# Feed-forward gate and up as one 512-column product: both halves of the input side by side, summed by VectorE

## The reference

```python
D_FF = 2816
def swiglu(xn, w_gate, w_up, w_down):
    return (jax.nn.silu(xn @ w_gate) * (xn @ w_up)) @ w_down
h = h + swiglu(rmsnorm(h, ffn_norm[l]), w_gate[l], w_up[l], w_down[l])   # l = 0, 1
```

## Time and profile before

| | us |
|---|---|
| median of 3 runs | 1963.29 (1955.23 to 1964.63) |
| profiled execution | 1963.11 |
| its span | 1961.3 |
| TensorE busy | 1734.0 (88%) |
| VectorE busy | 1019.6 (52%) |
| ScalarE busy | 510.2 (26%) |

### The profile page before, as it was taken

One profiled execution on the slowest core, in us unless ns is written; L12 is line 12 of the kernel. 1 busy time (PEld: TensorE's weight loads), 2 busy tenths in 40 slices (PEclk: granted clock), 3 DMA queues, 4 the chain that ended last, 5 costly groups with the idle time before them and its releaser, 6 DMA issues.

```text
span 1961.3 us, 22190 instructions
## 1 busy us (share of the span) xinstructions
PE 1734.0 (88%) x7497; PEld 1181.4 (60%) x7497; DVE 1019.6 (52%) x2438; ACT 510.2 (26%) x1012; POOL 279.1 (14%) x264
## 2 busy tenths in 40 slices
PE   7998999889989999799999899968878889788876
PEld 4784999856648999587565468543434434344332
DVE  1234555533435554445734311377776667776765
ACT  1342444212324443143211001122222212222222
POOL 0000000000000000000000000045434343333540
PEclk8999999999998999899999999989989999898998
DMA  5253566501336565133322325099999999999996
GB/s 173 77 169 103 167 192 183 167 16 44 96 103 181 180 184 182 31 126 124 105 110 80 115 78 189 25 371 420 420 421 421 422 421 421 421 421 421 422 421 255
DMA packets 209713, 435.30 MB, mean 222 GB/s; under 512 B 11649, under 2 KB 145153, under 8 KB 175745
## 3 DMA queue, kind: packets, MB, share of 16 engines
q0 software_dynamic: 36864, 268.45, 33.0%
q1 hardware_dynamic: 171760, 166.06, 26.5%
q10 hardware_dynamic: 1040, 0.13, 0.0%
HBM read 433.53 MB, written 1.05 MB: 222 GB/s over the span
## 4 chain that ended last, share of the span: by engine, by line
PE 72%; DMA 16%; DVE 7%; issue 3%; ACT 1%; POOL 0%; DVEq 0%; SPq 0%; POOLq 0%; ACTq 0%
PE ps L484 40%; DMA OT<-in_peer_uv,IX 15%; PE ps L1220 11%; PE ps L645 6%; PE ps L925 3%; PE ps L938 2%; PE ps L515 2%; PE ps L549 1%; PE ps L490 1%; PE ps L1135 1%; DVE SLOT L2277 1%; PE ps L1017 1%; DVE AR L1992 1%; PE ps L556 1%; DMA XT<-in_w_pq_by_head 0%
## 5 line engine op out<-in xcount | busy, mean ns | idle before, releaser
L1595 POOL DMA_INDIRECT SLOT<-in_peer_uv,IX x128 | 136.1, 1064 | 1520.2 <-DVE IX L2271 1276.0
L1220 PE MATMUL ps<-SLOT,AR 128*128 128x512 f32 x512 | 263.8, 671 | 96.6 <-ACT AR L1549 96.6
L484 PE MATMUL ps<-ARH 128*128 128x256 f32 x2112 | 261.0, 286 | 7.6 <-DVE ARH L1710 7.6
L484 PEld LDWEIGHTS ps<-ARH 128*128 128x128 f32 x2112 | 260.2, 195 | 9.5 <-issue 7.9
L1220 PEld LDWEIGHTS ps<-SLOT,AR 128*128 128x128 f32 x512 | 108.1, 216 | 245.9 <-issue 129.6
L2277 DVE SCALAR_TENSOR_TENSOR SLOT<-SLOT,V 128x1024 f32<-128x1024 f32 x128 | 153.3, 1224 | 77.4 <-DMA SLOT<-in_peer_uv,IX 75.4
L484 PE MATMUL ps<-XT,SLOT 128*128 128x256 f32 x832 | 183.2, 380 | 2.2 <-DVE XT L1659 1.3
L1710 DVE TENSOR_TENSOR ARH<-SLOT,ARH 128x2048 fp32r<-128x2048 f32 (+1 forms) x88 | 154.1, 1756 | 49.3 <-ACT ARH L1298 32.5
L484 PEld LDWEIGHTS ps<-XT,SLOT 128*128 128x128 f32 x832 | 157.4, 190 | 25.2 <-issue 3.7
L1220 PE MATMUL ps<-AR 128*128 128x512 f32 x320 | 144.6, 601 | 12.1 <-ACT AR L1549 12.1
L484 PE MATMUL ps<-SLOT,XT 128*128 128x512 f32 (+3 forms) x384 | 148.5, 547 | 4.0 <-DVE XT L1659 2.6
(11 more groups left out here) (338 smaller groups left out, 2119.4 us busy)
## 6 DMA issues: line engine op xcount, KB each, us to landing
SLOT<-in_w_gate SPq DMA_DIRECT2D x44, 512.0 KB, 4.0
SLOT<-in_w_up SPq DMA_DIRECT2D x44, 512.0 KB, 5.3
SLOT<-in_w_down SPq DMA_DIRECT2D x44, 512.0 KB, 5.2
SLOT<-in_w_in SPq DMA_DIRECT2D x9, 2048.0 KB, 8.6
SLOT<-in_fox_w_in SPq DMA_DIRECT2D x16, 512.0 KB, 3.9
XT<-in_w_pq_by_head SPq DMA_DIRECT2D x8, 1024.0 KB
SLOT<-in_mla_w_uq SPq DMA_DIRECT2D x8, 576.0 KB
SLOT<-in_fox_w_in SPq DMA_DIRECT2D x2, 2048.0 KB, 13.2
```

The lines of the kernel that those rows point to most:

```text
L484: m = pe.matmul(outp, l, r, start=(n_ == 0), stop=(n_ == len(pairs) - 1))
L1220: m = pe.matmul(ps[:, 2 * t + c, :], DIAG[:, j, :], v_row(j)[:, c * 512:(c + 1) * 512], start=False, stop=False)
L1595: pool.indirect_dma_start(PAIR[j], None, pairs, bass.IndirectOffsetOnAxis(IX[:, t, j:j + 1], 0)).then_inc(gathered[j], 16)
```

## The change

In TensorE's list a gate or up product has a bank of its own (4 + 2b + g). Per chunk there are two matmuls: the weights' high part by both parts of the input side by side, 512 columns; and the weights' low part by the input's high part, 256 columns, into the first half of the bank. VectorE copies the second half of the bank to SBUF (SG for gate, the now unused XT for up), adds the first half to it and tells ScalarE (gate_summed, up_summed). Silu works in SBUF. ScalarE starts the next weights' high part only after up_summed, where before silu's own wait stood for both products. The down product waits for hidden_ready instead of the bank's release.

```diff
                         for g in range(2):
-                            m = group(ps[:, 4 + b, g * S:(g + 1) * S],
-                                      sum((thirds(lambda h: WGU[:, b, h, g, k, :], lambda h: XH[:, h, k, :]) for k in range(KC)), []))
-                        m.then_inc(full["a"][4 + b], 1)
-                        T.add(free["v"][4 + b])
+                            o_ = 4 + 2 * b + g
+                            take(o_)
+                            for k in range(KC):
+                                pe.matmul(view(ps[:, o_, :], 2, S), WGU[:, b, 0, g, k, :], XH[:, :, k, :], start=(k == 0), stop=False)
+                                m = pe.matmul(ps[:, o_, 0:S], WGU[:, b, 1, g, k, :], XH[:, 0, k, :], start=False, stop=(k == KC - 1))
+                            m.then_inc(full["v"][o_], 1)
+                            T.add(free["v"][o_])
                     for b in range(2):
                         pe.wait_ge(sem(f"dn_split{b}"), T.next(sem(f"dn_split{b}")))
-                        evacuated(4 + b)
+                        pe.wait_ge(sem("hidden_ready"), T.next(sem("hidden_ready")))
...
             def gated(b):
-                act.wait_ge(full["a"][4 + b], T.next(full["a"][4 + b]))
-                act.activation(SG[:, b, :], ps[:, 4 + b, 0:S], ACT.Silu).then_inc(sem("silu_ready"), 1)
+                act.wait_ge(sem("gate_summed"), T.next(sem("gate_summed")))
+                act.activation(SG[:, b, :], SG[:, b, :], ACT.Silu).then_inc(sem("silu_ready"), 1)
+                act.wait_ge(sem("up_summed"), T.next(sem("up_summed")))
...
             def gated(b):
+                for g, dst, told in ((0, SG[:, b, :], "gate_summed"), (1, XT[:, b, :], "up_summed")):
+                    o_ = 4 + 2 * b + g
+                    dve.wait_ge(full["v"][o_], T.next(full["v"][o_]))
+                    dve.tensor_copy(dst, ps[:, o_, S:2 * S]).then_inc(chain, 1)
+                    dve.wait_ge(chain, T.next(chain))
+                    TT(dst, dst, ps[:, o_, 0:S], ALU.add).then_inc(free["v"][o_], 1)
+                    T.add(free["v"][o_])
+                    settled(o_)
+                    signal(told)
                 dve.wait_ge(sem("silu_ready"), T.next(sem("silu_ready")))
-                TT(SG[:, b, :], SG[:, b, :], ps[:, 4 + b, S:2 * S], ALU.mult).then_inc(chain, 1)
+                TT(SG[:, b, :], SG[:, b, :], XT[:, b, :], ALU.mult).then_inc(chain, 1)
                 dve.wait_ge(chain, T.next(chain))
                 dve.tensor_copy(HT[:, b, 0, :], SG[:, b, :]).then_inc(chain, 1)
                 dve.wait_ge(chain, T.next(chain))
-                low(HT[:, b, 1, :], SG[:, b, :], HT[:, b, 0, :]).then_inc(free["v"][4 + b], 1)
-                T.add(free["v"][4 + b])
+                low(HT[:, b, 1, :], SG[:, b, :], HT[:, b, 0, :]).then_inc(sem("hidden_ready"), 1)
```

More of the change, by code:

```diff
@@ L630, in blocks @@
                         pe.wait_ge(sem(f"gu_split{b}"), T.next(sem(f"gu_split{b}")))
-                        take(4 + b)
                         for g in range(2):
-                            m = group(ps[:, 4 + b, g * S:(g + 1) * S],
-                                      sum((thirds(lambda h: WGU[:, b, h, g, k, :], lambda h: XH[:, h, k, :]) for k in range(KC)), []))
-                        m.then_inc(full["a"][4 + b], 1)
-                        T.add(free["v"][4 + b])
+                            o_ = 4 + 2 * b + g
[5 more added lines that the diff above has]
+                            T.add(free["v"][o_])
                     for b in range(2):
                         pe.wait_ge(sem(f"dn_split{b}"), T.next(sem(f"dn_split{b}")))
-                        evacuated(4 + b)
+                        pe.wait_ge(sem("hidden_ready"), T.next(sem("hidden_ready")))
                         for t in range(NT):
@@ L2354 @@
         free_a2=1, free_v5=1),
-    "pe:ffn0": dict(gu_split0=1, free_v4=1, gu_split1=1, free_v5=1, dn_split0=1, dn_split1=1),
+    "pe:ffn0": dict(gu_split0=1, free_v4=1, free_v5=1, gu_split1=1, free_v6=1, free_v7=1, dn_split0=1, hidden_ready=2,
+        dn_split1=1),
     "pe:mla": dict(free_v1=1, free_v2=1, slot_here0=16, free_a0=1, slot_here1=16, free_a6=1, free_v7=1, probs_ready=2, free_a3=1,
         free_a4=1, free_a2=1, free_v5=1),
-    "pe:ffn1": dict(gu_split0=1, free_v4=1, gu_split1=1, free_v5=1, dn_split0=1, dn_split1=1),
+    "pe:ffn1": dict(gu_split0=1, free_v4=1, free_v5=1, gu_split1=1, free_v6=1, free_v7=1, dn_split0=1, hidden_ready=2,
+        dn_split1=1),
     "pe:sb": dict(free_v1=1, free_v2=1, slot_here0=16, slot_here1=16, free_a0=1, keep_ready=2, free_v3=1, free_v4=1, free_a6=1,
@@ L2364 @@
     "act:fox": dict(max_ready=2, full_a0=1, full_a6=1, full_a3=1, full_a4=1, full_a2=1),
-    "act:ffn0": dict(full_a4=1, raw_here0=32, full_a5=1, raw_here1=32, raw_here2=16, dn_used0=1, raw_here3=16, dn_used1=1),
+    "act:ffn0": dict(gate_summed=2, up_summed=2, raw_here0=32, raw_here1=32, raw_here2=16, dn_used0=1, raw_here3=16, dn_used1=1),
     "act:mla": dict(max_ready=2, full_a0=1, full_a6=1, full_a3=1, full_a4=1, full_a2=1),
-    "act:ffn1": dict(full_a4=1, raw_here0=32, full_a5=1, raw_here1=32, raw_here2=16, dn_used0=1, raw_here3=16, dn_used1=1),
+    "act:ffn1": dict(gate_summed=2, up_summed=2, raw_here0=32, raw_here1=32, raw_here2=16, dn_used0=1, raw_here3=16, dn_used1=1),
     "act:sb": dict(absz_ready=2, act_chain=2, full_a0=1, expo_ready=2, full_a6=1),
@@ L2371 @@
     "dve:fox": dict(full_v1=1, free_v1=1, full_v2=1, free_v2=1, probs_ready=2, dve_chain=1, full_v5=1, free_v5=1),
-    "dve:ffn0": dict(silu_ready=2, dve_chain=4, free_v4=1, high_ready=4, free_v5=1),
+    "dve:ffn0": dict(full_v4=1, dve_chain=8, free_v4=1, full_v5=1, free_v5=1, silu_ready=2, high_ready=4, full_v6=1, free_v6=1,
+        full_v7=1, free_v7=1),
     "dve:mla": dict(full_v1=1, free_v1=1, full_v2=1, free_v2=1, full_v7=1, dve_chain=2, free_v7=1, probs_ready=2, full_v5=1,
         free_v5=1),
-    "dve:ffn1": dict(silu_ready=2, dve_chain=4, free_v4=1, high_ready=4, free_v5=1),
+    "dve:ffn1": dict(full_v4=1, dve_chain=8, free_v4=1, full_v5=1, free_v5=1, silu_ready=2, high_ready=4, full_v6=1, free_v6=1,
+        full_v7=1, free_v7=1),
     "dve:sb": dict(full_v1=1, free_v1=1, full_v2=1, free_v2=1, ln_ready=2, dve_chain=2, full_v3=1, free_v3=1, full_v4=1,
@@ L2378 @@
     "dve:cross": dict(full_v1=1, free_v1=1, probs_ready=1, dve_chain=1, full_v4=1, free_v4=1),
-    "dve:peer": dict(gathered0=32, gathered1=32, gathered2=32, gathered3=32, gate_exp=2, dve_chain=32, gathered4=32, gathered5=32,
-        gathered6=32, gathered7=32, gelu_ready=8, gathered8=32, gathered9=32, gathered10=32, gathered11=32, gathered12=32,
+    "dve:peer": dict(gathered0=32, gathered1=32, gathered2=32, gathered3=32, gate_exp=2, dve_chain=32, gelu_ready=8, gathered4=32,
+        gathered5=32, gathered6=32, gathered7=32, gathered8=32, gathered9=32, gathered10=32, gathered11=32, gathered12=32,
         gathered13=32, gathered14=32, gathered15=32, full_v7=1, free_v7=1, best_ready=2),
```

## The result

| | before | after |
|---|---|---|
| median of 16 runs each, us | 1955.58 | 1969.12 |
| ratio after to before | | 1.0045 (95%: 1.0031 to 1.0059) |
| profiled execution / its span, us | 1963.11 / 1961.3 | 1963.5 / 1961.7 |
| turn of the feed-forward loop, us | 16.98 | 17.33 |

What follows compares the result with a forecast made beforehand. TensorE was taken to bound the feed-forward; 20 turns at +0.115 us, less two gains of 0.38, gave +1.5 us on 1963.3, forecast 1965 us. Range 1955 to 1974 us, the forecast's own 1960 to 1970 at chance 0.66.

Steps and rivals of the forecast that it cites:

- The centre I gave, +1.5 us: Both feed-forwards: 20 turns 0.115 us longer each, two last turns 0.38 us shorter each, together +1.5 us.
- up 0 full: Gate and up product: block 0's up bank is filled 5.565 us after the turn's start.
- copy of up 0 to the hidden block 1 done: VectorE and ScalarE from up 0's copy at 5.605 us to block 1's low part ending at 14.05 us.
- The mechanism: Down product: TensorE waits for hidden block 1, as gate 1's copy queues behind VectorE's 2.29 us low part; 0.50 us a turn.
- The sign that I had named: Down line: a new TensorE wait for VectorE's low part, 20 to 22 times at about 0.4 to 0.5 us.
- The product's term: Gate and up matmuls: fewer, wider instructions save 0.38 us a turn, 8.4 us over 22 turns.
- the sign that the term was wrong: Gate and up piece of 64 matmuls: 11.4 us or more a turn, not 11.1, would refute the product's saving.
- The chain: One turn's sequence through VectorE and ScalarE, from up 0 full to hidden block 1, making the turn 17.10 us.
- 1 (cover holds): Down product covers VectorE's work, no stall is left; -8.4 us, 1955 us, chance 0.12.
- 2: VectorE's chain becomes the bound at gate 1's copy behind the low part; +10.5 us, 1974 us, chance 0.12.
- 3 (nothing comes back from the product): Gate and up matmuls stay at 11.51 us, cost not per instruction; +6 us, 1969 us, chance 0.06.
- 4 (clock): TensorE's stalls let the granted clock fall, 1.7 us lost a turn; +36 us, 1999 us, chance 0.04.

Runs made afterwards that it cites:

- e2: Changed kernel with the old product of 96 matmuls a turn, keeping VectorE's copies and adds; turn 17.44 us, ratio to before 1.0088.
- e4: Changed kernel with VectorE's low part of the next gate and up weights moved behind both blocks' sums and hidden parts; turn 16.79 us, ratio to before 0.9991.
- e6: Changed kernel with only gate 1's sum moved ahead of VectorE's low part of the next weights; turn 17.09 us, ratio to before 1.0015.
- e5: Changed kernel with low parts behind both blocks and each product's eight wide matmuls before its eight narrow ones; turn 16.61 us, ratio to before 0.9961.
- e1: Changed kernel without VectorE's sums, silu and multiply reading PSUM directly as before the change; turn 16.79 us, ratio to before 0.9972.
- e7: Repeat of e4, the changed kernel with the next weights' low parts behind both blocks; turn 16.79 us, ratio to before 0.9974.
- e3: Changed kernel with the input's two parts adjacent in SBUF, so 512 columns are one run; turn 17.34 us, ratio to before 1.0041.

## Why the prediction was right, and in what size it was off

The forecast was 1965 us with no change beyond 0.5%, in 1955 to 1974; measured were 1969.12 and +0.45%. The interval, 0.31 to 0.59%, reaches over the 0.5% that I had set, so this came out near the edge. The centre I gave, +1.5 us, was too small by some 6 us as the two stages show it and by 7 as the whole kernel does. That 1965 lies only 4 us from the measured time is luck in part: I had added the 1.5 to 1963.3, the median of three runs, and that of sixteen is 1955.6.

| step | predicted | after |
|---|---|---|
| up 0 full, from the turn's start | 5.565 | 5.66 |
| copy of up 0 to the hidden block 1 done | 8.45 | 8.59 |
| weight load after it | +0.05 | +0.04 |
| twelve wide matmuls from the restart | 3.00 | 3.01 |
| turn | 17.10 | 17.33 |

**The mechanism was right.** The wait on hidden_ready ends last; gate 1's copy stands right behind the 2.29 us low part (its told-copy at 250.75, the copy at 250.81). e2 has the stall without the product, e4 takes it away by order alone, and e6 takes away a part of it. In size the stop was 0.54 us (17.33 against 16.79 without it), where I had 0.50. The sign that I had named, 20 to 22 waits in the down line, came 20 times, listed at 0.26 to 0.30 us and not 0.4 to 0.5; the last section says where the rest is.

**The product's term was too large.** I had 0.38 us a turn, and it is 0.19: gate and up take 11.3 us, between the 11.1 that I expected and the 11.4 that I had named as the sign that the term was wrong. The wide and narrow spacings that I took, 0.228 and 0.120, hold only in runs of one width, as e5 shows: a pair is 0.349 there and 0.3535 where the widths alternate (16 pairs in after from 257.07 to 262.73, 5.66 us). With 14 fewer changes of width in eight pairs, one change costs some 3 ns. I had bounded this term from nothing to 10.3 us and taken 8.4 from rows of a like but unmixed stream. In the changed kernel, where the chain sets the turn, the late 0.09 of up 0 went straight into the turn.

**The chain was 0.14 us too short.** The told-copy of up 0 ends at 246.49 and ScalarE starts at 246.60, 0.11 later; I had 0.03, from hops whose releaser was a plain result. After a told-copy that is followed by a wait VectorE also starts 0.10 us later, not 0.07 (252.69 to 252.79). That is 0.11 of the 0.14; the rest, 0.03, is spread over the other hops.

Both errors have the same sign: 0.09 + 0.14 = 0.23 us a turn. The sum then is 20 x 0.35 - 2 x 0.19 = +6.6 us, against some 7.2 in the two stages at a like start (the second layer's turns are 17.36 and not 17.33, which is 0.3 of it) and 6.1 to 11.5 for the whole kernel. What stands between 7.2 and the centre of 8.8 lies within the interval; the runs don't tell it from chance.

**Rivals.** 1 (cover holds) is out: ten stops a layer. 2 has the right place, and a third of its extra lateness came true. 3 (nothing comes back from the product) is out by e1, though it was half right in size. 4 (clock) is out: the granted clock is 1.00 in both stretches with a stop in every turn. The clock does cost something at the start of each stage, but in both kernels, as told above.

**The figure of the Trainium skill.** The Trainium skill (TensorE: Matmul & The Clock Gate, "Wait — 56ns, not 53.3ns?") gives some 2.5 ns beside the columns per warm matmul. Here a removed matmul with its weight load gave back 0.19/32 = 6 ns in the mixed stream and (16.98 - 16.61)/32 = 12 ns grouped, so the traces disagree with the figure: it is too small for this fp32r stream, in which every matmul loads new weights. Whether the format or the weight loads make the difference no run shows. By it the turn would be an estimated 16.90 at best, and e5 ran 16.61.

## What to carry to other kernels

When work is added to an engine that is half idle, count where it stands in that engine's list, not its busy time: 3.9 us a turn were free in one order (e4, e7) and cost 0.54 in another. The cheap remedy is to place a long job that nobody awaits soon behind the short ones that somebody does. And in a turn set by a chain through other engines, time saved on the busiest engine counts only as far as it lies ahead of that chain (e2 against after).

## What the runs showed of the hardware that I had not expected

- A stop of TensorE costs more than the gap in its matmul row. e6 loses 0.30 us a turn with 0.2 us of matmul waits in the whole first layer; after loses 0.54 with about 0.26 listed. Two things are missing from the list. The gap is counted from the last matmul's modelled end, 0.16 us after the next one would have started in an unbroken stream (255.98 against 256.14 in before); and the first matmul after a stop lasts up to 0.50 us, where the median of its line is 0.39. In the turn shown 0.24 + 0.16 + 0.11 = 0.51 of the 0.54. The weight loads' row is the better measure: before the load that had to wait it is idle for 0.43 us in e6, 0.59 in e2 and 0.66 in after, and the losses are 0.30, 0.48 and 0.54.
- Alternating between 512 and 256 columns costs about 3 ns a change (e5 against e4 and e7: 0.18 us a turn for 56 changes fewer); whether by the width, by the part of the bank that is written or by the change of operands was not told apart.
- A 512-column operand read as two runs of 256 is as fast as one run (after and e3: 17.33 and 17.34 us a turn).
